# A hybrid layer and two mixer layers on one core: one half of a 31-tap convolution moved to GpSimd, the softmaxes of layer 2 in two PSUM halves, row spreads as transposes

## What is computed

```python
def conformer_conv(a_val, a_gate, conv_w, conv_b, ln_g, ln_b):
    glu = a_val * jax.nn.sigmoid(a_gate)
    y = depthwise_conv(glu, conv_w) + conv_b          # 31 taps, 256 channels
    return jax.nn.silu(layer_norm(y, ln_g, ln_b))

# diff_attention, per block of 128 queries and per head (4 heads)
p1 = softmax(q1 @ k1.T * scale)
p2 = softmax(q2 @ k2.T * scale)
o = (p1 - lam * p2) @ v                               # then rms_norm over the head

def token_mixers(z, ...):
    y_a = conformer_conv(a_val, a_gate, ...)
    y_b = diff_attention(q1, q2, k1, k2, v, lam, ...)
    y_c = spatial_gating(u, sv, ...)
    y_d = short_conv_mixer(bg, cg, xin, conv_d_w)
    return concatenate([y_a, y_b, y_c, y_d]) @ w_out
```

## Time and profile before

| | before |
|---|---|
| median of three runs | 2074.77 us |
| lowest and highest | 2065.75 and 2076.05 us |
| the profiled execution | 2064.61 us |
| its span in the profile | 2062.0 us |
| VectorE busy | 1274.8 us, 62% |
| ScalarE busy | 795.7 us, 39% |
| DMA, mean | 122 GB/s |

### The profile page before, as it was taken

How to read it: one execution, slowest core, us unless ns; L and a number is a source line. 1 busy time by engine, 2 the same in 40 slices (tenths; PEclk the granted TensorE clock), 3 DMA queues, 4 the chain that set the end, 5 groups by cost and what they waited for, 6 DMA issues and landing times. The chain is left out here.

```text
span 2062.0 us, 26692 instructions
## 1 busy us (share of the span) xinstructions
PE 2011.9 (98%) x11220; PEld 1714.4 (83%) x11220; DVE 1274.8 (62%) x1704; ACT 795.7 (39%) x1138; POOL 72.5 (4%) x81
## 2 busy tenths in 40 slices
PE   7999999999999999999999999999998999999998
PEld 6989888778888988788888888888886788888887
DVE  7466765876757996737546455464798746344443
ACT  4333334495343365534122122132536634232231
POOL 0000000000030000030000000001100010000001
PEclk9999999999999999999999999999999999999999
DMA  8543533634422531223223232232353132222221
GB/s 310 214 163 123 187 120 113 208 108 162 179 92 78 171 103 72 72 92 115 103 103 122 92 123 103 104 130 106 111 171 93 72 107 88 102 84 100 102 100 64
DMA packets 55623, 250.76 MB, mean 122 GB/s; under 512 B 6512, under 2 KB 12800, under 8 KB 37328
## 3 DMA queue, kind: packets, MB, share of 16 engines
q1 hardware_dynamic: 53472, 244.38, 34.3%
q0 software_dynamic: 592, 2.46, 0.3%
q10 hardware_dynamic: 1440, 2.24, 0.3%
HBM read 232.00 MB, written 12.06 MB: 118 GB/s over the span
## 5 line engine op out<-in xcount | busy, mean ns | idle before, releaser
L2144 PE MATMUL banks<-hxh,whi_f 128*128 128x512 f32 (+1 forms) x1464 | 580.5, 397 | 8.5 <-ACT hxh L2344 3.3
L2144 PE MATMUL banks<-hxh,wlo_f 128*128 128x512 f32 (+1 forms) x1464 | 568.1, 388 | 0.0
L2144 PE MATMUL banks<-hxl,whi_f 128*128 128x512 f32 (+1 forms) x1464 | 554.0, 387 | 0.2 <-DVE hxl L2604 0.2
L2525 DVE TENSOR_TENSOR wlo_f<-raw_f,whi_f 128x2048 fp32r<-128x2048 f32 x128 | 293.6, 2294 | 174.5 <-ACT whi_f L2304 174.3
L2304 ACT ACTIVATE whi_f<-raw_f 128x2048 fp32r<-128x2048 f32 x130 | 248.0, 1908 | 294.3 <-PE banks L2144 276.1
L2144 PEld LDWEIGHTS banks<-hxh,whi_f 128*128 128x128 f32 x1464 | 276.2, 189 | 74.6 <-issue 21.3
L2144 PEld LDWEIGHTS banks<-hxh,wlo_f 128*128 128x128 f32 x1464 | 275.6, 188 | 57.8
L2144 PEld LDWEIGHTS banks<-hxl,whi_f 128*128 128x128 f32 x1464 | 274.5, 188 | 54.5 <-DVE hxl L2604 0.9
L2144 PE MATMUL banks<-fxh,whi_f 128*128 128x512 f32 (+1 forms) x528 | 202.6, 384 | 0.0
L2144 PE MATMUL banks<-fxh,wlo_f 128*128 128x512 f32 (+1 forms) x528 | 202.5, 384 | 0.0
L2144 PE MATMUL banks<-fxl,whi_f 128*128 128x512 f32 (+1 forms) x528 | 202.5, 384 | 0.0
(11 more groups left out here) (354 smaller groups left out, 3117.4 us busy)
## 6 DMA issues: line engine op xcount, KB each, us to landing
raw_f<-in_wst SPq DMA_DIRECT2D x133, 1024.0 KB, 4.9
mvr<-in_mst SPq DMA_DIRECT2D x120, 512.0 KB, 5.8
stack<-qk_parts SPq DMA_DIRECT2D x36, 192.0 KB, 6.6
x_kept<-xT SPq DMA_DIRECT2D x2, 2048.0 KB, 9.5
raw_f<-in_wst SPq DMA_DIRECT2D x8, 384.0 KB, 5.7
xT<-x_kept SPq DMA_DIRECT2D x2, 1536.0 KB, 9.5
qk_parts<-qk_h SPq DMA_DIRECT2D x3, 768.0 KB, 3.8
qk_parts<-qk_l SPq DMA_DIRECT2D x3, 768.0 KB, 3.9
```

What stands on the lines that cost most here:

```text
L2144: last = pe.matmul(o, (wh, wl)[w][:, k, c, :], r[part][:, k, :], start=(k == order[0] and parts is not LOW and (w, part) == (0, 0)), stop= ...
L2525: dve.tensor_tensor(wlo[r][:], raw[r][:], whi[n % 2 if n > N_FIRST else n][:].bitcast(F32), ALU.subtract).then_inc(w_lo, 1)
```

## The change

Four things change; the rest stays in its order.

1. The convolution. VectorE's `conv` issues the 31 taps of channel tile 0 alone, 15, 9 and 7 in layer 1 and 11, 14 and 6 in layer 2, all before the units; none stays in the units. GpSimd's new `conv` issues tile 1 as a `tensor_scalar` into `tapped` and a `tensor_tensor` into `aconv` for each tap, each waiting for the one before. Its loads for the gating stand behind the 14th tap (layer 1) or the 18th (layer 2). `means` waits for both.
2. Layer 2's units. The accumulators of j = 5 to 9 shrink to one bank each, and the two score halves get two banks each. Each half has its own matmuls (`scores_part`, the second one place later), its own maximum, and its own release after its exponential. VectorE's order is first maximum of v + 1, combine(v), second maximum. Turns, values and joins stand one place later, save for the last unit of each stretch.
3. All spreads are `transpose` instead of `matmul`.
4. The start. ScalarE's queue loads its tiles of x before `c1b`, squares five tiles instead of four before it takes the silu, and TensorE's first sums use a column of ones set by a memset and wait for the constants only at the spread.

```diff
 class Plan:
+    def later(self, v):
+        return self.wait * (v not in (self.cut - 1, self.units - 1))
     def turned(self, v):
-        return self.start(v) + (2 if self.second(v) else 3)
+        return self.start(v) + (2 if self.second(v) else 3) + self.later(v)
...
+            def scores_part(v, i):
+                h, j = v // p.per, v % p.per
+                st = stack[h % 2]
+                q, o = st[:, i, j * P:(j + 1) * P], parted[1][i]
+                if i and v:
+                    pe.wait_ge(q_e, p.part_done(v - 1, 1))
+                pe.matmul(o[:, 0:T], q, st[:, 2 + i, 0:T], start=True, stop=True)
+                pe.matmul(o[:, T:TX], q, st[:, 2 + i, T:TX], start=True, stop=True).then_inc(q_s, 1)
...
 # means, on TensorE
-                pe.wait_ge(conv_step, CONV_STEPS * (l + 1))
+                pe.wait_ge(conv_step, TAPS_A * (l + 1))
+                pe.wait_ge(conv_half, 2 * TAPS_A * (l + 1))
...
 # conv, on VectorE
-                    tap, c = taps[0] // 2, taps[0] % 2
-                        dve.wait_ge(conv_step, CONV_STEPS * l + taps[0] - 1)
+                        dve.wait_ge(conv_step, TAPS_A * l + tap)
-                    conv((9, 11)[j - 3] if two else (14, 13)[j - 3])
+                    conv((9, 7)[j - 3] if two else (14, 6)[j - 3])
...
 # run, on VectorE
                     if v + 1 < v1:
                         upto(p.scores(v + 1))
+                        if p.parts == 2:
+                            maxima(v + 1, 0)
                     combine(v)
                     if v + 1 < v1:
-                        maxima(v + 1)
-                    splits = unit_weights(1 if two else 2)
-                    if v0 == 0:
-                        conv((1 if two else 0) if splits else 2)
+                        maxima(v + 1, p.parts - 1)
+                    unit_weights(1 if two else 2)
...
 # GpSimd
+            def conv(l, first, end):
+                wc = XPA - 30 if l == 0 else T
+                if first == 0:
+                    pool.wait_ge(w_lo, C_L + l * N_L + 3 + 1 - N_FIRST)
+                for tap in range(first, end):
+                    w, src = vcol(f"caw{l}", TAPS_A + tap, 1), gpad[:, 1, tap:tap + wc]
+                    if tap:
+                        pool.wait_ge(conv_half, 2 * (TAPS_A * l + tap))
+                    if tap == 0:
+                        pool.tensor_scalar(aconv[:, 1, 0:wc], src, w, vcol(f"cab{l}", 1, 1), ALU.mult, ALU.add
+                                           ).then_inc(conv_half, 2)
+                    else:
+                        pool.tensor_scalar(tapped[:, 0:wc], src, w, None, ALU.mult).then_inc(conv_half, 1)
+                        pool.wait_ge(conv_half, 2 * (TAPS_A * l + tap) + 1)
+                        pool.tensor_tensor(aconv[:, 1, 0:wc], aconv[:, 1, 0:wc], tapped[:, 0:wc], ALU.add
+                                           ).then_inc(conv_half, 1)
+                conv(l, 0, (14, 18)[l])
                 pool.wait_ge(roped, 4 * l + 4)
                 pool.dma_start(wsT[:], sgw[l]).then_inc(ld_sg, 16)
                 pool.dma_start(bsg[:], sgb[l]).then_inc(ld_sg, 16)
+                conv(l, (14, 18)[l], TAPS_A)
...
 # norm_spread; half_spread and spread alike
-                    last = pe.matmul(d.bc[:, j * P:(j + 1) * P], d.rs[:, j:j + 1].to_broadcast([P, P]), ident,
-                                     start=True, stop=True)
+                    last = pe.transpose(d.bc[:, j * P:(j + 1) * P], d.rs[:, j:j + 1].to_broadcast([P, P]), ident)
...
 # the start, on ScalarE
-            act.dma_start(c1b[:], cbt[0]).then_inc(ld_c1, 16)
             for i in (1, 3):
                 act.dma_start(xT[:, 2 * i:2 * i + 2, :], xrs[:, 2 * i:2 * i + 2, :]).then_inc(ld_x[i], 16)
+            act.dma_start(c1b[:], cbt[0]).then_inc(ld_c1, 16)
```

More of the change, by code:

```diff
@@ L44 @@
 XPD = TX + 4
-CONV_STEPS = 2 * TAPS_A
 QSCALE = 32 ** -0.5
@@ L176, in __init__ @@
         self.o0, self.pair0 = 12 * l, 8 * l
+        self.parts = 1 + l
+        self.wait = l
     def start(self, v):
@@ L729, in means @@
                 for g in range(4):
-                    half, o = 64 * (g % 2), 1024 + P * (g // 2)
-                    last = pe.matmul(score[half:half + 64, o:o + P], ones[:, 0:64], wsT[:, g, :], start=True, stop=True)
+                    half, o = 64 * (g % 2), taps_at[l] + P * (g // 2)
+                    last = pe.matmul(mixing[l][half:half + 64, o:o + P], ones[:, 0:64], wsT[:, g, :], start=True, stop=True)
                 last.then_inc(m_mean, 1)
@@ L768, in fill @@
                         scores(v)
+                    if l and g == p.scores(v) + 1:
+                        scores_part(v, 1)
                     if g == p.values(v) and (p.second(v) or p.context(v)):
@@ L1039, in exp @@
                 upto(p.scores(v))
+                if part < p.parts:
+                    act.wait_ge(q_m, p.part_done(v, part))
                 if part == 0:
-                    act.wait_ge(q_m, u0 + v + 1)
                     if v >= 2:
@@ L1053, in exp @@
                                              bias=dnm[:, z + o:z + o + 1], accum_out=dls[:, z + o:z + o + 1])
-                if part:
+                if part or p.parts == 2:
                     ins.then_inc(q_e, 1)
@@ L1535, in sub_norm, with run @@
                 ins.then_inc(o_n, 1)
-            def run(v0, v1, more=0, late=()):
-                maxima(v0)
+            def run(v0, v1, late=()):
+                for part in range(p.parts):
+                    maxima(v0, part)
                 weights_due()
@@ L1555, in run @@
                 fresh[0] = False
-            run(0, p.cut, CONV_STEPS - taps[0] - 2 * p.cut)
-            conv(CONV_STEPS)
+            run(0, p.cut)
             def by_row(col):
@@ L1591, in layer_dve @@
             dve.wait_ge(gelus, 2 * l + 2)
-            for i, (c, ps) in enumerate(((1, score), (0, turned))):
+            for i, (c, ps) in enumerate(((1, mixing[l]), (0, turned[l]))):
                 dve.wait_ge(s_mix, 2 * l + i + 1)
@@ L1872, in bring_back @@
                 p = PLAN[l]
-                sync.wait_ge(q_s, p.u0 + p.per * (3 + part))
+                sync.wait_ge(q_s, p.parts_done(p.per * (3 + part)))
                 k = slice(6, KT) if part else slice(0, 6)
```

129 lines of the change are left out of this document (74 added, 55 removed).

## The result

| | before | after | after less before |
|---|---|---|---|
| first comparison, median | 2075.41 us (6 runs) | 2089.11 us (6 runs) | +13.7, ratio 1.0077 (95% 1.0051 to 1.0103) |
| second comparison, median | 2076.77 us (17 runs) | 2098.30 us (5 runs) | +21.5, ratio 1.0112 (95% 1.0090 to 1.0135) |
| execution profiled first | 2064.61 us | 2089.51 us | +24.9 |

The change makes the kernel slower, by 0.8 to 1.1%. The forecast was 2121 us. The ledger further down compares two executions of the same pace.

A forecast was written before the change was run, and what follows sets the result against it. TensorE, busy 98% of the span, was taken as the bound, with VectorE close behind in the projections. Port exclusion 67, layer 1's attention -1, layer 2's softmaxes -11, spreads -5, start -4: +46 on 2074.77, 2121 us, range 2105 to 2155.

The forecast's parts named there:

- The bound and the mechanism: Projections: TensorE bounds, VectorE has 3.3 and 3.0 us in hand; two-SBUF-input instructions exclude GpSimd's; chance 0.66.
- Rival 1: Convolution: GpSimd's half costs VectorE nothing, taps stay below 1.1 us; 2052 us, chance 0.23.
- Rival 2: Convolution: VectorE keeps the port, GpSimd gets what is left and the means come late; about 2075 us, chance 0.11.
- Rival 3: Layer 2's softmaxes: ScalarE's queue holds an equally long ring, so 11 us less are won; no separate chance given.
- the price of the 43 instructions: Before each layer's first maximum: 43 VectorE instructions each wait for one GpSimd instruction; maxima 43.6 and 23.6 us later.
- it reads half as much: GpSimd's one-input multiplication: half the addition's time per column, 0.85 us at 798 columns and 0.545 at 512.
- The cover of the units: Layer 1's attention: freed VectorE wins back about 2.5 us, remaining GpSimd turns cost 1.5; net -1 us.
- The ring of layer 2: Layer 2's softmax units: 5.25 us each falls to about 4.3; 11 us won, bounds 5 and 14.
- Start and spreads: Earlier first sums: -4 us, bounds 0 and -5; 44 identity matmuls made transposes: -5 us, bounds 0 and -6.
- The base: Whole kernel: the median 2074.77 us of the runs before, to which +46 us was added.
- the two bounds for the multiplication: GpSimd's multiplication at 798 columns: hold of 0.56 us from VectorE's one-input instruction, 1.70 from GpSimd's addition.
- the lower bound of the whole: TensorE's loss before both layers' first maxima: 67 us, bounds 57 and 97.

The follow-up runs named there:

- `add_only`: Changed kernel with GpSimd's multiplications for the second convolution tile left out, only its additions kept (result not the convolution): 2095.9 us.
- `taps_moved`: Changed kernel with 13 of VectorE's taps in layer 1 and 9 in layer 2 moved into the attention units: 2080.93 us, 1.0019 of before.
- `banks_only`: Kernel before with only layer 2's own softmax banks and the order that goes with them: 2068.30 us, 0.9959 of before.
- `conv_only`: Kernel before with only the convolution split between VectorE and GpSimd, and two semaphores merged: 2115.22 us, 1.0175 of before.
- `late`: Changed kernel, VectorE doing 35 and 38 taps before the attention, GpSimd only the second tile's last 14 and 12 from the first maximum: 2057.49 us, 0.9904.

## Why the prediction was right and wrong

**The bound and the mechanism: right.** TensorE without a gap and VectorE with 3.3 us in hand was the reading that decided the sign. The shared port was read from two meetings in the trace of before; in the changed kernel 21 of the 30 taps in layer 1's stage and 20 of 30 in layer 2's took longer than alone. So the engines do not meet only at semaphores, as the opening has it: no semaphore stands between these taps and GpSimd's. Rival 1 (no exclusion; taps below 1.1 us) falls by the 1684 ns. Rival 2 (VectorE keeps the port) falls by the alternation in `add_only`, though its price, GpSimd late for the mean, is what `taps_moved` met. Rival 3 falls by `banks_only`. The rule of the Trainium skill (SBUF — State Buffer, section "SBUF: two separate sides"), that the shared port is an exclusive lock held for the whole instruction, gives the right sign and the wrong size: by it a multiplication of 2.9 us would shut out a VectorE tap for all of its length, and the rows show a wait of 0.55 us.

**The step that failed: the price of the 43 instructions.** The sum charged each with one GpSimd instruction of 1.275 us in layer 1, 54.8 us in all and 50.8 net of the fixed parts. Measured in the same stretch: 30 taps cost 50.5 - 30 x 0.97 = 21.4, the rotation steps 4 x 0.94 + 4 x 0.40 = 5.4, the low parts 0.7, the splits 0: 27.5 us, 0.64 each. Less the 4 taps saved (3.9) and 0.6 of idle time filled (2.7 left of 3.3), that is the measured +23.0. In layer 2, 12.6 + 2.3 + 1.1 = 16.0 where 31.3 was forecast; less 4.7, +11.3 against +10.3. (The 1.0 us left over in layer 2 is not accounted for.) The causes, in rows. The changed kernel repeats itself every 5.0 us in its run of taps, of which this is one round:

```profile
654.13 1.05 DVE L1398 SCALAR_TENSOR_TENSOR aconv<-gpad,vecs,aconv 128x798 f32<-128x798 f32 x1
654.71 1.93 POOL L1996 TENSOR_TENSOR aconv<-aconv,tapped 128x798 f32<-128x798 f32 x1
655.22 2.27 DVE L1398 SCALAR_TENSOR_TENSOR aconv<-gpad,vecs,aconv 128x798 f32<-128x798 f32 x1
656.74 2.91 POOL L1994 TENSOR_SCALAR tapped<-gpad,vecs 128x798 f32<-128x798 f32 x1
657.52 1.60 DVE L1398 SCALAR_TENSOR_TENSOR aconv<-gpad,vecs,aconv 128x798 f32<-128x798 f32 x1
659.15 1.05 DVE L1398 SCALAR_TENSOR_TENSOR aconv<-gpad,vecs,aconv 128x798 f32<-128x798 f32 x1
```

Three VectorE taps pass for each GpSimd tap, not two. They pay 1.22, 0.55 and 0. First, the count: not each of the 43 waits. While a multiplication lasts 2.9 us and shuts VectorE out for 0.55 of them, one tap waits and the next passes free, so 30 GpSimd instructions met the stage and not 43. Second, the addition's hold is 1.22 us, where 1.70 was worked out from its length at 512 and 256 columns. The line through those two was too steep: alone, the tap's addition takes 1.09 us at 512 columns, where the sum of squares took 1.29, and 1.60 at 798, where the line gives 1.90; why two additions of one form differ stays open. And part of the 1.60 us does not shut VectorE out. Third, the multiplication was placed by "it reads half as much". As a duration that is far off, 2.3 to 2.9 us where I took 0.85 and the upper bound was 1.70, and the estimate of 0.69 that stands beside it in the prediction is further off still; as a hold it is off the other way, 0.55. The two are different numbers, and I had taken one for both. By count and size together, 15 x (1.22 + 0.55) = 26.6 us, against the 27.5 measured.

**The cover of the units: wrong in sign.** Forecast -1, measured +5.2, and `conv_only` has the same +5.2. TensorE's waits for the exponentials in layer 1's attention are 8.1 us where before had 3.0. The largest part is the one wait of 3.68 us before the second scores: it comes from the late first maximum, so it is more of the stage's loss, which the mark at 725.39 cuts off. The prediction let the first maximum's lateness be all that TensorE loses, and had 1.5 us of turns behind it. GpSimd also still had half of its taps to do, and its chain went on to 796 us; `late` and `taps_moved`, whose first maxima are in time, wait 5.2 and 5.8 us for the exponentials with GpSimd beside the units. How the rest of the 5.2 us is made up is not shown.

**The rest: right within 3 us.** The ring of layer 2 (forecast 4.3 us for 5.25) is 4.45 us in the changed kernel, the mean of eleven between two reciprocals, of which this one is 4.65:

```profile
1610.28 0.16 DVE L1547 RECIPROCAL small<-small 128x2 f32<-128x2 f32 x1
1610.47 0.22 DVE L1548 SCALAR_TENSOR_TENSOR small<-small 128x1 f32<-128x1 f32 x1
1610.73 1.80 DVE L1553 SCALAR_TENSOR_TENSOR prob<-prob,small 128x768 f32<-128x768 f32 x1
1612.45 0.94 DVE L1530 TENSOR_REDUCE small<-banks 128x1 f32<-128x768 f32 x1
1614.06 0.96 DVE L1530 TENSOR_REDUCE small<-banks 128x1 f32<-128x768 f32 x1 [0.66 <-PE banks L711]
1614.93 0.15 DVE L1547 RECIPROCAL small<-small 128x2 f32<-128x2 f32 x1
```

against the earlier trace rows; the first half's maximum (1614.06) runs ahead of the reciprocal, in the shadow of the exponentials, and the second half's (1612.45) behind the combination. Gain 9.8 of 11. Start and spreads gave 7.4 of 9 in the ledger (its first, fourth and last stretch), 8 by their own run; no run tells the spreads from the start. TensorE at the start, against the earlier trace rows:

```profile
12.77 2.48 PE L2234 MATMUL banks<-small,nsq 128*128 128x1 f32 x11
15.91 1.09 PE L2115 MATMUL banks<-consts,small 128*128 128x128 f32 x4 [0.66 <-DVE small L2619]
19.37 0.76 PE L2201 MATMUL banks<-hxh,whi_f 128*128 128x512 f32 x1 [2.37 <-ACT hxh L2402]
```

The first projection comes 2.45 us earlier, not 4, since the sums end at 15.25 and not at 13.2. The prediction let them end a quarter of their 6.99 us after the last pair of squares. They began at 8.29, with the first pair, and took 6.96 us in all, so that was too early for them whatever the last pair did.

**The base.** 46 us on the median 2074.77 gave 2121, with a range from 2105 to 2155; both medians of the changed kernel, 2089 and 2098, lie below it, and 21.5 was measured in the place of 46. No point between the two bounds for the multiplication (0.56 and 1.70) could have hit it: the hold lies at the lower end and the duration above the upper one, and even the lower bound of the whole, 57 in the place of 67, gives +36. The loss was mis-sized by more than its own bounds allowed, because the count of 43 had no bound of its own.

## What to carry to other kernels

Before work is given to GpSimd, look at whether the stretch is VectorE's: here 35 and 38 taps lay wholly beside TensorE's matmuls, so the split had nothing to win, and cost 39 us alone (`conv_only`). Where both engines read SBUF tiles, price a GpSimd instruction by two numbers, how long it lasts and how long it shuts VectorE out, and charge VectorE once per GpSimd instruction, not GpSimd once per VectorE instruction. The parts of a change can have opposite signs: without the convolution this one is 0.9% faster than before, with it 1% slower.

## What the runs showed of the hardware

- GpSimd's one-input multiplication by a scalar per row takes longer than its two-input addition: alone 2.29 and 1.60 us at 798 columns, 1.56 and 1.09 at 512. These rows stand near the chain's end in layer 1, with VectorE hardly in the way:

```profile
787.68 2.29 POOL L1994 TENSOR_SCALAR tapped<-gpad,vecs 128x798 f32<-128x798 f32 x1
790.06 1.60 POOL L1996 TENSOR_TENSOR aconv<-aconv,tapped 128x798 f32<-128x798 f32 x1
```

- The granted clock of TensorE falls after it has stood idle. In the changed kernel:

```profile
680.00:690.00 10.00, 4.94 (x17) 3.22 (x15) 8.38 (x6) 4.68 (x4) 9.64 (x5) 0.66 0.34 106
690.00:700.00 10.00, 10.00 (x84) 9.94 (x83) 9.79 (x7) 0.00 (x0) 9.64 (x5) 1.00 0.72 236
700.00:710.00 10.00, 6.42 (x54) 6.21 (x52) 9.86 (x9) 1.82 (x2) 9.63 (x5) 0.98 0.00 0
710.00:720.00 10.00, 6.49 (x27) 6.07 (x28) 9.89 (x6) 4.15 (x4) 9.73 (x6) 0.50 0.83 251
```

  A clock of 0.50 is 1.2 GHz of 2.4. TensorE was busy for 62.85 us in the stage where 53.0 did, so about 10 of the 23 us show as a slower TensorE. I take them for no cost of their own: VectorE was busy for 72.3 of the 75 us and grew by 23.7, and TensorE stood idle again at the end of the stage, for 3.68 us, so it would have waited at any clock. No run here holds the clock up to show it.
- Executions have one of two paces of TensorE, 579 or 568 matmuls in 100 us at a granted clock of 1.00, 10 us apart in the whole: from the mark behind layer 1's attention to layer 2's low parts three of the twelve traces take 603.8 to 605.4 us and nine take 613.3 to 616.1. What sets it stays open. Both profiles that were compared first had the quicker pace, while most runs of before had the slower, and the first comparison put the change at +13.7 us where executions of one pace differ by 21 to 25 (2076.7 to 2097.84, and 2064.61 to 2089.51).
